# In the last stage of a one-core encoder step, the shift of every odd tile is added by GpSimd in place of VectorE

## The chip, the cores and the metric

The kernel runs on one core of one Trainium2 chip. The metric is the device time of one execution in microseconds (us); a measurement gives the median of several runs, and beside it one execution is recorded by the hardware profiler.

## What is computed

The reference is one inference step of a hybrid encoder layer for two request groups: a prompt of 2048 rows and a sample of 64 rows, each row 1024 float32 numbers wide. There is a modulated RMSNorm, one input projection to a state-space branch and a forgetting-attention branch, an output projection, a second modulated RMSNorm and a mixture of sixteen experts. After the layer comes a final modulated RMSNorm, and only that is touched here:

```
mod_p = (jax.nn.silu(c_prompt) @ w_ada_f + b_ada_f)[:, None, :]
sh_p, sc_p = jnp.split(mod_p, 2, axis=-1)
y_prompt = rmsnorm(yp, final_norm_w) * (1 + sc_p) + sh_p      # and the same for the sample group
```

So each row x of the layer's output becomes x * rs * scale + shift. Here rs is one over the root of the mean of the row's squares plus 1e-6, scale is final_norm_w * (1 + sc), and shift is sh. The scale and the shift are the same for all rows of one group.

## The kernel before

The kernel is a chain of stages (modulation, the state-space branch with the input projection, the forget sums, the projection to queries, keys and values, attention, output projection, routing, experts, `final`). Each stage is a block with one instruction stream per engine and semaphores between the streams. There is a barrier between stages, so `final` starts only when the experts have ended, and nothing follows it.

`final` works on 17 tiles of 128 rows (the last has 64), tile i = 0 to 16. SyncE's queue loads tile i into slot i % 8 of `x3` (L2437); from tile 8 on it first waits until the tile eight places earlier has been scaled. ScalarE squares the tile and sums the squares (`square`, L2449). VectorE makes the mean of one column (`mean`, L2477), ScalarE takes its root (L2454), and VectorE takes the reciprocal (L2482). VectorE then makes x * rs * scale into slot i % 4 of `out` (L2486, called the scaling here) and, after a wait on its own semaphore `scaled`, adds the shift in place (L2489, called the add). ScalarE's queue stores the slot to the result (`store`, L2459). The scaling of tile i waits until the store of tile i - 4 has landed, because it reuses its slot.

The scale rows and the shift rows lie in SBUF as `c.last_rows`. So the scaling has two whole tiles as inputs in SBUF (`x3` and the scale rows), and so has the add (`out` and the shift rows).

The order on each engine is written out by hand, and each engine works strictly in that order. The two loops that matter are:

```
# ScalarE
for i in range(NT):
    if i + 1 < NT:
        square(i + 1)
    take_root(i)
    if i >= 1:
        store(i - 1)
# VectorE
for i in range(NT):
    if i + 1 < NT:
        mean(i + 1)
    normalize(i)
```

A store waits on ScalarE for the add of its tile, so the square of the next tile but two stands behind that wait. GpSimd has no instruction in `final`.

Four other places of the kernel are spoken of because their rows show GpSimd and VectorE at work at once. In the state-space branch GpSimd makes `yskip` (L607) and `xw` (L611) and VectorE makes `xdt` (L683). In the forget sums GpSimd takes three of the differences `wb_lo` (L877) while VectorE runs sums along rows (L888 to L894). In attention GpSimd adds up `c_acc` (L1391), each time in place: accumulator plus a tile, all in SBUF and float32. In the experts GpSimd copies two numbers per row to `x_wg` (L2200).

Of the kernel before, what the change touches and what calls it, by code (L numbers as in the profile page):

```python
# [10 lines left out]
ALU = mybir.AluOpType  # L11
# [9 lines left out]
NT = NT_P + 1  # L21
# [31 lines left out]
def stage_semaphores(nc, ctx, prefix):  # L53

    handles = []

    def give_back():
        nc.clear_and_free_semaphores(handles)
        nc.all_engine_barrier()

    ctx.callback(give_back)

    def sem(name):
        handles.append(nc.alloc_semaphore(prefix + name))
        return handles[-1]

    return sem
# [7 lines left out]
def load_functions(nc, act, table):  # L75
    act.add_instruction(mybir.InstLoadActFuncSet(name=nc.get_next_instruction_name(), act_func_set_id=table, ins=[], outs=[]))
# [2340 lines left out]
def final(nc, c, a):  # L2417

    RING, RING_OUT = 8, 4
    with ExitStack() as ctx:  # L2420
        sb = lambda n, s, d=F32: ctx.enter_context(nc.sbuf_tensor("z_" + n, s, d))
        sem = stage_semaphores(nc, ctx, "z_")
        x3, out, junk = sb("x3", [P, RING, D]), sb("out", [P, RING_OUT, D]), sb("junk", [P, 2, D])
        st = sb("st", [P, NT, 4])
        ssq, ms, root, rs, scaled, out_ready = map(sem, ("ssq", "ms", "root", "rs", "scaled", "out_ready"))
        x_loaded, stored = [sem(f"x_loaded{s}") for s in range(RING)], [sem(f"stored{s}") for s in range(RING_OUT)]
        block = ctx.enter_context(nc.Block())
        rows_of = lambda i: P if i < NT_P else DEC
        group_of = lambda i: 0 if i < NT_P else 1

        @block.sync
        def _(sp):
            def load(i):
                n = rows_of(i)
                if i >= RING:
                    sp.wait_ge(scaled, i - RING + 1)
                sp.dma_start(x3[0:n, i % RING], c.x2[i * P:i * P + n, :]).then_inc(x_loaded[i % RING], 16)  # L2437

            for i in range(NT):
                load(i)  # L2440

        @block.scalar
        def _(act):
            load_functions(nc, act, SQRT)

            def square(i):
                n = rows_of(i)
                act.wait_ge(x_loaded[i % RING], 16 * (i // RING + 1))
                act.activation(junk[0:n, i % 2], x3[0:n, i % RING], ACT.Square, accum_out=st[0:n, i, 0:1]).then_inc(ssq, 1)  # L2449

            def take_root(i):
                n = rows_of(i)
                act.wait_ge(ms, i + 1)
                act.activation(st[0:n, i, 2:3], st[0:n, i, 1:2], ACT.Sqrt).then_inc(root, 1)  # L2454

            def store(i):
                act.wait_ge(out_ready, i + 1)
                dst = a["y_prompt"][0, i * P:(i + 1) * P, :] if i < NT_P else a["y_sample"][0]
                act.dma_start(dst, out[0:rows_of(i), i % RING_OUT]).then_inc(stored[i % RING_OUT], 16)  # L2459

            square(0)
# [6 lines that stand above are left out]
            store(NT - 1)  # L2468
            for s in range(RING_OUT):
                act.wait_ge(stored[s], 16 * len(range(s, NT, RING_OUT)))  # L2470

        @block.vector
        def _(dve):
            def mean(i):
                n = rows_of(i)
                dve.wait_ge(ssq, i + 1)
                dve.tensor_scalar(st[0:n, i, 1:2], st[0:n, i, 0:1], 1.0 / D, EPS, ALU.mult, ALU.add).then_inc(ms, 1)  # L2477

            def normalize(i):
                n, s, o, g = rows_of(i), i % RING, i % RING_OUT, group_of(i)  # L2480
                dve.wait_ge(root, i + 1)
                dve.reciprocal(st[0:n, i, 3:4], st[0:n, i, 2:3]).then_inc(rs, 1)  # L2482
                dve.wait_ge(rs, i + 1)
                if i >= RING_OUT:
                    dve.wait_ge(stored[o], 16 * (i // RING_OUT))
                dve.scalar_tensor_tensor(out=out[0:n, o], in0=x3[0:n, s], scalar=st[0:n, i, 3:4], in1=c.last_rows[0:n, g, 0, :],  # L2486
                                         op0=ALU.mult, op1=ALU.mult).then_inc(scaled, 1)
                dve.wait_ge(scaled, i + 1)
                dve.tensor_tensor(out[0:n, o], out[0:n, o], c.last_rows[0:n, g, 1, :], ALU.add).then_inc(out_ready, 1)  # L2489

            mean(0)
            for i in range(NT):
# [3 lines that stand above are left out]
# [6 lines left out]
def build(nc, a):  # L2502
    c = Shared()
    with ExitStack() as ctx:
# [45 lines left out]
        with ExitStack() as held:  # L2550
            weights = ExpertWeights(nc, held, a)
            routing(nc, c, a, weights)
            experts(nc, c, a, weights)
        final(nc, c, a)


# [28 lines left out]
```

## Time and profile before

| what | us |
|---|---|
| median of 3 runs | 2740.62 |
| lowest and highest of them | 2738.66, 2743.02 |
| the profiled execution, its own time | 2734.53 |
| its span from the first to the last instruction | 2732.8 |
| first load of `final` issued, by the span's clock | 2677.01 |
| last store of `final` issued | 2728.92 |

The profiled execution is a single one, and it was 6.09 us shorter than the median. The stage `final` takes the last 55.8 us of its span. Times inside the trace are given from the span's start; durations of one instruction are in us in an order of time and in ns where a view says mean or min/median/max. PE is TensorE, DVE is VectorE, ACT is ScalarE, POOL is GpSimd and SP is SyncE; a q behind a name is that engine's queue of issued transfers.

### The profile page before, as it was taken

The numbers are of one execution on the slowest core, as the hardware profiler recorded it, in microseconds if no ns is written. First come the engines' busy times: TensorE is split into PE (matmuls) and PEld (weight loads), VectorE is DVE, ScalarE is ACT, GpSimd is POOL, SyncE is SP. The second block draws the span as 40 slices with busy tenths as digits, with TensorE's granted clock in tenths as the row PEclk, the third lists the DMA queues.
The fourth block names the chain that finished last, engine by engine and source line by source line (L and its number), as shares of the span: only waits on it lengthen the run. The fifth ranks groups of instructions, "written<-read, shape, count | busy, mean of one in ns | idle before, by whom it ended". The sixth has DMA issues, their size and how long they took to land. (4 is left out here: it accounts for less than half of the span.)

```text
span 2732.8 us, 34773 instructions
## 1 busy us (share of the span) xinstructions
PE 2308.2 (84%) x11435; PEld 1788.9 (65%) x11436; DVE 1390.9 (51%) x2752; ACT 944.3 (35%) x1622; POOL 706.1 (26%) x753
## 2 busy tenths in 40 slices
PE   3799999739999979999995999708999999999870
PEld 1688888626778845556553888506888888888650
DVE  1488887761110056666663565531445662434556
ACT  1344444321111125555555343211223441223433
POOL 0010001020000057777774000051222222223220
PEclk8899999869999969999997999858999999999985
DMA  6421211146764294445522444315657776457656
GB/s 195 156 76 61 75 73 54 49 166 228 262 249 155 93 213 84 84 84 107 114 40 93 133 145 133 139 66 169 175 160 242 247 242 193 139 151 240 230 184 261
DMA packets 190201, 407.36 MB, mean 149 GB/s; under 512 B 65275, under 2 KB 72873, under 8 KB 186689
## 3 DMA queue, kind: packets, MB, share of 16 engines
q1 hardware_dynamic: 161152, 304.05, 34.6%
q0 software_dynamic: 26576, 93.53, 12.5%
q10 hardware_dynamic: 2384, 8.65, 0.8%
q8 instruction: 48, 0.79, 0.1%
q14 instruction: 41, 0.33, 0.0%
HBM read 296.12 MB, written 110.07 MB: 149 GB/s over the span
## 5 line engine op out<-in xcount | busy, mean ns | idle before, releaser
L1391 POOL TENSOR_TENSOR c_acc<-c_acc,c_pr 128x512 f32<-128x512 f32 (+3 forms) x320 | 340.4, 1064 | 73.4 <-ACT c_pr L1513 32.6
L1513 ACT ACTIVATE c_pr<-c_ps,neg_f 128x512 f32<-128x512 f32 (+2 forms) x360 | 207.8, 595 | 160.7 <-PE c_ps L1457 153.8
L1543 DVE TENSOR_REDUCE c_mx<-c_pm 128x1 f32<-128x512 f32 (+3 forms) x304 | 178.7, 613 | 57.4 <-PE c_pm L1413 39.4
L1413 PE MATMUL c_pm<-c_km,c_q 66*128 66x512 f32 (+1 forms) x336 | 143.8, 444 | 22.2 <-DMA c_km<-f_k 15.8
L258 PE MATMUL p_zx<-wa_hi,ah_hi 128*128 128x432 f32 x408 | 154.6, 379 | 3.6 <-DVE ah_lo L640 3.6
L258 PE MATMUL x_pg<-x_g_hi,x_x_hi 128*128 128x512 f32 x336 | 136.0, 405 | 23.9 <-DVE x_x_lo L2360 23.9
L1176 DVE SCALAR_TENSOR_TENSOR b_lo<-b_pu,b_hi 128x512 fp32r<-128x512 f32 (+1 forms) x40 | 24.5, 612 | 257.2 <-ACT b_hi L1145 257.2
L1466 PE MATMUL c_po<-c_pr,c_vv 128*64 128x512 f32 (+3 forms) x720 | 150.9, 521 | 0.0
L607 POOL TENSOR_TENSOR yskip<-xs,params 128x512 f32<-128x512 f32 x17 | 21.9, 1287 | 497.5 <-ACT xs L545 497.5
L259 PE MATMUL p_zx<-wa_lo,ah_hi 128*128 128x432 f32 x408 | 149.3, 366 | 0.0
L260 PE MATMUL p_zx<-wa_hi,ah_lo 128*128 128x432 f32 x408 | 148.6, 364 | 0.0
L258 PE MATMUL x_pd<-x_d_hi,x_m_hi 128*128 128x512 f32 x344 | 140.8, 409 | 6.8 <-DVE x_m_lo L2370 6.8
L2215 POOL DMA_INDIRECT x<-x_out,x_dst x43 | 75.5, 1755 | 268.1 <-DVE x_out L2378 262.3
L1451 PE MATMUL c_ps<-c_q,c_k 128*128 128x512 f32 (+2 forms) x360 | 135.9, 379 | 2.8 <-DMA c_vv<-in_cache_v_dram 2.8
L259 PE MATMUL x_pd<-x_d_lo,x_m_hi 128*128 128x512 f32 x344 | 137.3, 399 | 0.0
L260 PE MATMUL x_pd<-x_d_hi,x_m_lo 128*128 128x512 f32 x344 | 137.1, 399 | 0.0
L258 PE MATMUL x_pu<-x_u_hi,x_x_hi 128*128 128x512 f32 x336 | 136.5, 406 | 0.0
L1457 PE MATMUL c_ps<-c_q,c_k 97*128 97x512 f32 (+2 forms) x360 | 135.5, 378 | 0.5 <-DVE c_q L1569 0.5
L259 PE MATMUL x_pg<-x_g_lo,x_x_hi 128*128 128x512 f32 x336 | 135.2, 402 | 0.0
L260 PE MATMUL x_pg<-x_g_hi,x_x_lo 128*128 128x512 f32 x336 | 135.1, 402 | 0.0
L260 PE MATMUL x_pu<-x_u_hi,x_x_lo 128*128 128x512 f32 x336 | 133.3, 397 | 0.0
L259 PE MATMUL x_pu<-x_u_lo,x_x_hi 128*128 128x512 f32 x336 | 133.2, 396 | 0.0
(389 smaller groups left out, 5606.3 us busy)
## 6 DMA issues: line engine op xcount, KB each, us to landing
x_raw_g<-in_w_gate_dram SPq DMA_DIRECT2D x32, 1024.0 KB, 8.9
x_raw_u<-in_w_up_dram SPq DMA_DIRECT2D x32, 1024.0 KB, 7.3
x_raw_d<-in_w_down_dram SPq DMA_DIRECT2D x32, 1024.0 KB, 6.8
b_wa<-in_w_ada_dram POOLq DMA_DIRECT2D x16, 1024.0 KB, 7.6
c_k<-k_hi SPq DMA_DIRECT2D x14, 672.0 KB, 13.7
h_hi<-ah_hi SPq DMA_DIRECT2D x17, 512.0 KB, 2.6
h_lo<-ah_lo SPq DMA_DIRECT2D x17, 512.0 KB, 3.5
d_mix<-mix SPq DMA_DIRECT2D x17, 512.0 KB
```

Source lines behind the costliest of these rows:

```text
L258: pe.matmul(out, a_hi, b_hi, start=start, stop=False)
L259: pe.matmul(out, a_hi, b_lo, start=False, stop=False)
L260: return pe.matmul(out, a_lo, b_hi, start=False, stop=stop)
L1176: dve.scalar_tensor_tensor(out=lo[:, n % RING, 0:w], in0=bank_of(n)[:, 0:w], scalar=HD ** -0.5 if un["kind"] == "q" else 1.0, in1=hi[:, n ...
L1391: pool.tensor_tensor(acc[:, ci % 2, cols], acc[:, ci % 2, cols], pr[:, i % RING, cols], ALU.add).then_inc(acc_done, 1)
L1413: last = pe.matmul(p_m[x % 2][:, 0:w * P], q2[0:KR, s, u["tile"] * P:(u["tile"] + 1) * P], km[:, s, kc], start=True, stop=not masked)
L1451: pe.matmul(out[:, cols], k1[:, s, kc], q1[:, s, qc], start=True, stop=False)
L1457: pe.matmul(out[:, cols], k2[0:ROW + 1, s, kc], q2[0:ROW + 1, s, qc], start=False, stop=True).then_inc(s_done, 1)
L1466: pe.matmul(p_o[ci % 2][half * HD:(half + 1) * HD, cols], vv[:, it["h"] % 2, it["key"], :], pr[:, i % RING, cols], start=it["kb"] < 2, sto ...
L1513: act.activation(pr[:, n % RING, cols], p_s[n % NPS][:, cols], ACT.Exp, bias=c.neg_f[:, it["h"], it["key"]:it["key"] + 1]).then_inc(exp_do ...
L1543: dve.tensor_reduce(mx[:, u % 2, pc["slot"]:pc["slot"] + 1], src, AX.X, ALU.max).then_inc(mx_done, 1)
L2215: nc.gpsimd.indirect_dma_start(out=c.x2, out_offset=bass.IndirectOffsetOnAxis(ap=dst[:, 0:1], axis=0), in_=out[:], in_offset=None, compute ...
```

## The change

GpSimd gets a stream in `final`: for the odd tiles 1, 3, ..., 15 it waits until the tile is scaled and adds the shift in place, in the same slot of `out`. VectorE adds the shift for the nine even tiles alone. The one semaphore `out_ready` becomes two, one for each adder, and ScalarE's store waits for the one of its tile's parity. Loads, squares, roots, scalings, rings and the order on ScalarE stay as they were.

```
-        ssq, ms, root, rs, scaled, out_ready = map(sem, ("ssq", "ms", "root", "rs", "scaled", "out_ready"))
+        ssq, ms, root, rs, scaled = map(sem, ("ssq", "ms", "root", "rs", "scaled"))
+        shifted = [sem("shifted_dve"), sem("shifted_pool")]
...
             def store(i):
-                act.wait_ge(out_ready, i + 1)
+                act.wait_ge(shifted[i % 2], i // 2 + 1)
...
+        @block.gpsimd
+        def _(pool):
+
+            for i in range(1, NT, 2):
+                n, o, g = rows_of(i), i % RING_OUT, group_of(i)
+                pool.wait_ge(scaled, i + 1)
+                pool.tensor_tensor(out[0:n, o], out[0:n, o], c.last_rows[0:n, g, 1, :], ALU.add).then_inc(shifted[1], 1)
...
-                dve.wait_ge(scaled, i + 1)
-                dve.tensor_tensor(out[0:n, o], out[0:n, o], c.last_rows[0:n, g, 1, :], ALU.add).then_inc(out_ready, 1)
+                if i % 2 == 0:
+                    dve.wait_ge(scaled, i + 1)
+                    dve.tensor_tensor(out[0:n, o], out[0:n, o], c.last_rows[0:n, g, 1, :], ALU.add).then_inc(shifted[0], 1)
```

## Rows read from the trace of the kernel before

**Rows 1.** Windows of `final`: engines' busy us, granted clock, DMA share, GB/s.
```profile
2695.00:2700.00 5.00, 0.00 (x0) 0.00 (x0) 4.86 (x9) 2.05 (x7) 0.00 (x0) 0.50 1.03 422
...
2715.00:2720.00 5.00, 0.00 (x0) 0.00 (x0) 4.86 (x9) 2.48 (x6) 0.00 (x0) 0.50 0.47 192
```

**Rows 2.** Instructions of `final` by line and form: busy us, mean ns | idle before.
```profile
L2486 DVE SCALAR_TENSOR_TENSOR z_out<-z_x,z_st,last_rows 128x1024 f32<-128x1024 f32 x16 | 20.6, 1285 | 0.6
L2489 DVE TENSOR_TENSOR z_out<-z_out,last_rows 128x1024 f32<-128x1024 f32 x16 | 19.6, 1225 | 0.6
```

**Rows 3.** Timeline of one steady tile of `final`: start us, duration us.
```profile
2704.73 1.28 DVE L2486 SCALAR_TENSOR_TENSOR z_out<-z_x,z_st,last_rows 128x1024 f32<-128x1024 f32 x1
...
2706.05 1.22 DVE L2489 TENSOR_TENSOR z_out<-z_out,last_rows 128x1024 f32<-128x1024 f32 x1
2707.19 0.14 DVE L2477 TENSOR_SCALAR z_st<-z_st 128x1 f32<-128x1 f32 x1
2707.25 0.15 DVE L2482 RECIPROCAL z_st<-z_st 128x1 f32<-128x1 f32 x1
...
2707.44 1.28 DVE L2486 SCALAR_TENSOR_TENSOR z_out<-z_x,z_st,last_rows 128x1024 f32<-128x1024 f32 x1
2707.69 1.06 ACT L2449 ACTIVATE z_junk<-z_x 128x1024 f32<-128x1024 f32 x1 [1.47 <-DVE z_out L2489]
2708.65 0.19 ACT L2449 ACTIVATION_READ_ACCUMULATOR z_junk<-z_x 128x1 f32 x1
2708.74 0.19 ACT L2454 ACTIVATE z_st<-z_st 128x1 f32<-128x1 f32 x1
```

**Rows 4.** Waits within `final`: us in total, times, longest.
```profile
ACT z_junk L2449 <- DVE z_out L2489: 19.8, 14, 1.5
```

**Rows 5.** Attention, GpSimd's first adds, timeline.
```profile
974.95 1.00 POOL L1391 TENSOR_TENSOR c_acc<-c_acc,c_pr 128x384 f32<-128x384 f32 x1 [0.92 <-ACT c_pr L1513]
976.44 0.72 POOL L1391 TENSOR_TENSOR c_acc<-c_acc,c_pr 128x256 f32<-128x256 f32 x1 [0.49 <-ACT c_pr L1513]
980.38 0.45 POOL L1391 TENSOR_TENSOR c_acc<-c_acc,c_pr 128x128 f32<-128x128 f32 x1 [3.22 <-ACT c_pr L1513]
...
987.40 1.27 POOL L1391 TENSOR_TENSOR c_acc<-c_acc,c_pr 128x512 f32<-128x512 f32 x1 [1.11 <-ACT c_pr L1513]
```

**Rows 6.** State-space branch, GpSimd at two tiles, timeline.
```profile
147.50 1.21 POOL L607 TENSOR_TENSOR yskip<-xs,params 128x512 f32<-128x512 f32 x1 [23.69 <-ACT xs L545]
149.34 1.04 POOL L611 TENSOR_TENSOR xw<-xdt,e_out 128x512 f32<-128x512 f32 x1 [0.63 <-DVE xdt L683]
...
174.87 1.55 POOL L607 TENSOR_TENSOR yskip<-xs,params 128x512 f32<-128x512 f32 x1 [24.48 <-ACT xs L545]
```

**Rows 7.** The same two tiles, VectorE, timeline.
```profile
147.06 0.75 DVE L627 TENSOR_SCALAR xn<-x,st 128x1024 f32<-128x1024 f32 x1
147.73 1.53 DVE L683 TENSOR_TENSOR xdt<-xs,dt 128x512 f32<-128x512 f32 x1
...
174.82 0.69 DVE L683 TENSOR_TENSOR xdt<-xs,dt 128x512 f32<-128x512 f32 x1 [1.06 <-ACT xs L545]
```

**Rows 8.** All of L683: durations in ns, min/median/max.
```profile
L683 DVE TENSOR_TENSOR xdt<-xs,dt x17: 691/1532/1535, 121.2 to 549.8; 128x512 f32<-128x512 f32 x17
```

**Rows 9.** Forget sums: GpSimd's first difference, durations in ns.
```profile
L877 POOL TENSOR_TENSOR wb_lo_early<-wb_raw_early,wb_hi x1: 7646/7646/7646, 571.6 to 571.6; 128x1536 fp32r<-128x1536 f32 x1
```

**Rows 10.** Forget sums, VectorE in the same stretch, timeline.
```profile
571.58 4.41 DVE L888 TENSOR_TENSOR_SCAN f_sum<-f_ones,scratch 8x2048 f32<-8x2048 f32 x1
...
576.74 3.57 DVE L892 TENSOR_TENSOR_SCAN f_sum<-f_ones,f_clt 8x512 f32<-8x512 f32 x1
580.34 3.45 DVE L894 TENSOR_TENSOR_SCAN f_sum<-f_ones,f_sum,scratch 8x128 f32<-8x128 f32 x1
```

**Rows 11.** Attention, timeline: VectorE's product with one input outside SBUF, beside GpSimd.
```profile
1043.42 5.54 POOL L1391 TENSOR_TENSOR c_acc<-c_acc,c_pr 128x512 f32<-128x512 f32 x4 [1.19 <-ACT c_pr L1513]
...
1047.84 0.42 DVE L1588 TENSOR_TENSOR c_orow<-c_px,c_rinv 128x256 f32<-128x256 f32 x1
```

**Rows 12.** All of L1588: durations in ns, min/median/max.
```profile
L1588 DVE TENSOR_TENSOR c_orow<-c_px,c_rinv x38: 223/424/425, 1015.4 to 1454.2; 128x256 f32<-128x256 f32 x31, 128x64 f32<-128x64 f32 x7
```

**Rows 13.** Stores of `final`, from issue to landing.
```profile
DMA to landing us min/median/max: 2.6/4.5/7.7
```

## The prediction

> **What bounds the kernel now.** I read the windows of the last stage first. In its middle VectorE is busy 4.86 of every 5.00 us, ScalarE about 2.05 and GpSimd not at all. The transfers run at a DMA share of 1.03 and 422 GB/s there, but late in the stage they fall to 0.47 and 192 GB/s, and VectorE is as busy as before [rows 1]. The transfers are dense, then, but they don't set the pace. The list by line says what VectorE does: 16 whole-tile scalings at a mean of 1285 ns and as many adds at 1225 ns, with 0.6 us of idle time before each group [rows 2]. The timeline of one tile gives the beat. One scaling starts at 2704.73 and the next at 2707.44, so a tile takes 2.71 us, and VectorE's instructions fill it: scaling, add, a mean and a reciprocal of one column [rows 3]. A scaling ends at 2704.73 + 1.285 = 2706.015; from there to the start of the next are **1.425 us**, which hold the add. That is what the change takes away after each odd tile. The table of waits shows that ScalarE is not the bound: 14 of its squares wait for an add, 19.8 us in total [rows 4]. These waits exist because each store stands in ScalarE's order ahead of a square, and that will matter below.
>
> If the odd adds cost VectorE nothing, eight times about 1.26 us (1.425 less the 0.165 us from the end of the add at 2707.275 to the next scaling, which stay) would go, 10.1 us. The question is what a GpSimd add costs VectorE.
>
> **The change, part by part.**
>
> *GpSimd's add.* The stage has no GpSimd row, so its price comes from attention, where GpSimd adds float32 tiles in place in SBUF, as here. Standing alone, 128, 256, 384 and 512 columns take 0.45, 0.72, 1.00 and 1.27 us [rows 5]: a straight line, 0.273 us for each 128 columns. From 512 to 1024 columns that adds 4 x 0.273 = 1.09, so **2.36 us**. The low bound is twice the 1.04 us that a product of 512 columns with a repeated factor took [rows 6], 2.08 us; the high one is twice 1.27, 2.54 us. I take 2.36, since operation, types and placement agree. The Trainium skill's GPSIMD Engine Reference, section 3.1 on elementwise work, gives about 2.6 cycles an element for a two-input operation at 1.2 GHz; an estimate from it is 2.22 us, and by that the sum below would be 5.9 us in place of 7.0.
>
> *Can it run beside VectorE?* In the state-space branch GpSimd's L607 starts at 147.50 and ends at 148.71; VectorE's L683, which reads two SBUF tensors, starts at 147.73 and needs 1.53 us [rows 6, 7]. One tile later VectorE starts first, needs 0.69 us, and now GpSimd's instruction is the long one, 1.55 us [rows 6, 7]. The one that comes second is stretched to past the end of the first, and over all 17 tiles L683 lies between 691 and 1535 ns with the median at 1532 [rows 8]. In the forget sums GpSimd's first difference takes 7.646 us [rows 9] beside a VectorE sum that ends at 571.58 + 4.41 = 575.99; what is left after that end is 3.24 us. And there a VectorE sum of 128 columns takes 3.45 us, hardly less than one of 512 columns at 3.57 [rows 10]: both ended when GpSimd let go. By contrast L1588, which has one input outside SBUF, took 0.42 us in the middle of a run of GpSimd adds [rows 11], and never over 425 ns in 38 instances [rows 12]. So a GpSimd instruction on SBUF and a VectorE instruction with two SBUF inputs take turns. In this stage the scaling and the add of VectorE both have two SBUF inputs, and every GpSimd add reads two. I therefore expect no overlap with the large work: after the odd tile's scaling GpSimd adds, and the next scaling waits for it.
>
> *The sum for one pair of tiles.* GpSimd starts 0.08 us after VectorE's result (L683 ends at 149.26, L611 starts at 149.34) [rows 6, 7]. The add takes 2.36. A held instruction saves part of its start: L683 ended 0.55 us after GpSimd's end at 148.71, where alone it needs 0.69, so 0.14 is given back [rows 6 to 8]. Does GpSimd come first? The next scaling needs a mean and a reciprocal before it, at least 0.165 us, against 0.08, and if it did not, the add would be held instead, the sum of the turns being the same. So from one scaling's end to the next start, 0.08 + 2.36 - 0.14 = 2.30 us take the place of 1.425: **+0.875 us** a pair. The pairs are (1,2) to (15,16), eight, so **+7.0 us**. Bounds by the price of the add: 2.08 gives 8 x 0.595 = +4.8, 2.54 gives 8 x 1.055 = +8.4.
>
> *What else changes.* The odd store now waits 0.08 + 2.36 us after the scaling, and behind it on ScalarE stand a square and a root. In steady state VectorE still has 1.145 + 0.04 + 1.225 + 0.165 = 2.58 us to do after GpSimd's end, the held scaling and the even add, before it needs that square. ScalarE needs 1.66 us for it: from the end of an add at 2707.27 over store issue and square to the end of the root at 2708.93 [rows 3]. So VectorE's turn hides it with 0.7 us to spare, after allowing 0.2 for the reciprocal. The ring of four output slots: an odd store is issued when GpSimd ends, the scaling that reuses its slot comes two pairs of 6.30 later less 3.7, some 8.9 us, and the slowest store landed after 7.7 [rows 13]; hidden. Loads wait for scalings, which come later, so they only find emptier transfers. The second semaphore adds no wait on VectorE; it loses one on odd tiles. The last tile is even and VectorE adds it, so the tail after it stays.
>
> Against the profiled execution the sum is 2734.53 + 7.0 = 2741.5 (span 2739.8). The median of the runs lies 6.09 us above that execution; nothing in the change speaks to that gap, so I carry it: 2740.62 + 7.0 = **2747.6**.
>
> **The rivals.**
>
> *The two do overlap (not slower).* If whole tiles of 1024 columns were interleaved and not held, VectorE alone would be done early, but ScalarE's order then sets the beat: odd scaling 1.285, GpSimd 0.08 + 2.36, then store, square and root 1.66, reciprocal and start of the next scaling some 0.23 [rows 3, 5]: 5.615 us a pair against 5.42 now. That is 8 x 0.195 = +1.6, 2742.2: no change. Against it stand all the pairs of rows 6 to 10. It decides once the even scaling starts under 2.11 us (1.425 + 0.69, with 0.69 an eighth of 5.5) after the odd one's end, in place of 2.30. 0.12.
>
> *VectorE is relieved (faster).* For a gain over 0.2%, 0.69 a pair, that same ScalarE beat must come under 4.73, so the add under 4.73 - 3.255 = 1.48 us with no hold. At the limit it is 10.1 us, 2730.5. The line of rows 5 speaks against it: 0.03.
>
> *The small mean is held too (slower still).* The mean of one column has its input and output in SBUF; its square is done 1.57 us after the even add's end (2707.27 to 2708.84) [rows 3], and GpSimd starts after 0.165 + 1.285 + 0.08 = 1.53. If it has to wait for GpSimd, the scaling behind it is not ready to go: the 0.14 is lost and mean, reciprocal and start, 0.165, come after: 8 x 0.305 = +2.4 more, +9.4, 2750.0. No row shows a one-column VectorE instruction beside a GpSimd add. A one-input instruction with everything in SBUF was at work when the L607 of 1.21 us began [rows 6, 7], and that is no proof. 0.15. The Trainium skill's SBUF — State Buffer, section "Who interferes with whom", says that a tensor_scalar can run in a mode with both port pairs and then shuts GpSimd out or waits for it; by that rule this rival is the case, and the time would be 2750.0.
>
> **How the numbers follow.** The difference that a measurement can tell from none is about 0.2%, 5.5 us. My forecast, turns with the mean free, has 0.67; the other cases have 0.12, 0.03 and 0.15, and 0.03 is left for costs that no row shows, such as a first add that is slow behind the experts' indirect transfers. The forecast's bounds are 2745.4 and 2749.0, and the bar for slower lies inside them at 2746.1; with the runs' own spread of some 2 us I give 0.50 of its 0.67 to slower. With the mean's 0.15 and the 0.03 that is 0.68 slower. Same takes the other 0.17 and the 0.12, 0.29. Faster 0.03. The range has to hold the two larger cases and the add at its bounds: the highest is 8.4 + 2.4 = +10.8, 2751.4, widened by the spread to 2752; down to 2742 it reaches the overlapping case.
>
> **What would show it.** GpSimd's adds near 2.36 us, starting some 0.08 us after an odd scaling; the even scalings recorded much longer than 1285 ns, with the odd ones and the nine adds unchanged; pairs at 6.3 us. VectorE's idle time stays small, since held time counts as busy. If the mean is held, the long row is the mean and not the scaling. If the two overlap, even scalings stay at 1285 ns, VectorE idles, and its idle time ends with ScalarE's square or root. The prediction is wrong on its main step if even scalings are short, and wrong on its size alone if the add is far from 2.36 us.

## The result, and the profile after

The changed kernel took 2747.56 us in the median of 12 runs (2742.47 to 2750.99), the kernel before 2739.53 us (12 runs, 2738.19 to 2743.02): a ratio of 1.0027 with a 95% interval of 1.0018 to 1.0036, so it is slower, by 4.9 to 9.9 us.

The profiled execution of the changed kernel took 2745.86 us with a span of 2744.2, 11.4 more than the span before. Not all of that belongs to the change. The first load of the last stage was issued at 2681.82, against 2677.01 before, and nothing ahead of that point was changed; in the runs below it lies anywhere from 2677.19 to 2686.55. I therefore compare the **stage length**, from that issue to the end of the span: 2744.2 - 2681.82 = 62.4 us after, 55.8 before, **+6.6 us**.

By line and form, the last stage after (busy us, mean ns | idle before), to be read against [rows 2]:

```profile
L2495 DVE SCALAR_TENSOR_TENSOR z_out<-z_x,z_st,last_rows 128x1024 f32<-128x1024 f32 x16 | 32.9, 2059 | 0.6
L2479 POOL TENSOR_TENSOR z_out<-z_out,last_rows 128x1024 f32<-128x1024 f32 x8 | 18.7, 2340 | 46.1 <-DVE z_out L2495 46.1
...
L2499 DVE TENSOR_TENSOR z_out<-z_out,last_rows 128x1024 f32<-128x1024 f32 x8 | 9.8, 1226 | 0.3
```

VectorE lost eight whole-tile adds of 1.2 us, 9.8 us in all, and its 16 whole-tile scalings grew from 20.6 to 32.9 us, 12.3 us. A mean hides where: the timeline of one pair shows it (start us, duration us), to be read against [rows 3]:

```profile
2715.56 1.28 DVE L2495 SCALAR_TENSOR_TENSOR z_out<-z_x,z_st,last_rows 128x1024 f32<-128x1024 f32 x1
...
2716.92 2.34 POOL L2479 TENSOR_TENSOR z_out<-z_out,last_rows 128x1024 f32<-128x1024 f32 x1 [3.87 <-DVE z_out L2495]
2716.99 0.15 DVE L2486 TENSOR_SCALAR z_st<-z_st 128x1 f32<-128x1 f32 x1
2717.08 0.16 DVE L2491 RECIPROCAL z_st<-z_st 128x1 f32<-128x1 f32 x1
2717.28 3.06 DVE L2495 SCALAR_TENSOR_TENSOR z_out<-z_x,z_st,last_rows 128x1024 f32<-128x1024 f32 x1
2720.38 1.23 DVE L2499 TENSOR_TENSOR z_out<-z_out,last_rows 128x1024 f32<-128x1024 f32 x1
...
2721.77 1.28 DVE L2495 SCALAR_TENSOR_TENSOR z_out<-z_x,z_st,last_rows 128x1024 f32<-128x1024 f32 x1
```

The odd scaling takes its 1.28 us. GpSimd starts 0.08 us behind its end and adds until 2719.26. VectorE's mean and reciprocal of one column, next in its order, keep their 0.15 us. The even scaling starts at 2717.28 on paper but ends only at 2720.34, 1.08 us behind GpSimd. A pair takes 2721.77 - 2715.56 = 6.21 us, against 2 x 2.71 before. VectorE shows hardly any idle time; the time that it is held is booked as work of the held instruction. In the 5 us from 2715 (busy us of TensorE, its weight loads, VectorE, ScalarE and GpSimd, then granted clock, DMA share, GB/s) VectorE counts as busy for 4.78 of 5.00 us:

```profile
2715.00:2720.00 5.00, 0.00 (x0) 0.00 (x0) 4.78 (x7) 1.56 (x4) 2.34 (x1) 0.50 0.55 202
```

That is how such a loss looks in a profile: one instruction of a kind more than twice as long as its fellows (3.06 us against 1.28), and no idle time to show for it.

### The profile page after: what moved, and what is told of

Read it like the earlier page. It is cut to its first block and busy times, and to the rows that moved or that the text cites. A ratio compares the mean times of both kernels' runs of the same rounds, so it can differ in the third digit from the quotient of the medians.

```text
span 2744.2 us, 34773 instructions
## 1 busy us (share of the span) xinstructions
PE 2310.1 (84%) x11435; PEld 1789.9 (65%) x11436; DVE 1397.4 (51%) x2744; ACT 944.4 (34%) x1622; POOL 725.3 (26%) x761
```

## The experiments

The theory is that of the prediction: a GpSimd instruction that reads SBUF and a VectorE instruction with two SBUF inputs take turns (the turns theory). The rivals are that GpSimd's latency or ScalarE's order sets the beat, or that any GpSimd work holds VectorE. All stage lengths are counted in the same way, from profiled executions; the beat is that of one steady pair of tiles, from one odd scaling to the next. The kernels of e3, e4, e5 and e7 to e10 were executed once each, so their rows rest on one execution. Whole times of single executions are not compared: the issue of the stage's first load alone moves by 9.4 us among the runs. (The 2741.42 us of e4 are below every run of the changed kernel, but there the stage began at 2677.19 and was as long.)

| run | stage, us | pair, us | even scaling, us |
|---|---|---|---|
| before | 55.8 | 5.42 | 1.28 |
| after | 62.4 | 6.21 | 3.06 |
| e1_memset | 56.3 | 5.57 | 1.28 |
| e2_no_odd_add | 51.0 | 4.98 | 1.28 |
| e3_side_add | 70.5 | 7.26 | 3.12 |
| e4_order | 62.5 | 6.21 | 3.33 |
| e5_psum | 56.3 | 5.60 | 1.28 |
| e6_psum_order | 46.8 | 4.16 | 1.28 |
| e7_before_psum | 55.8 | 5.42 | 1.28 |
| e8_small_extra | 46.7 | 4.15 | 1.28 |
| e9_wide_extra | 57.9 | 5.55 | 1.28 |
| e10_before_order | 56.4 | 5.42 | 1.28 |

**e1_memset: GpSimd as busy, but only writing.**

```
-                pool.tensor_tensor(out[0:n, o], out[0:n, o], c.last_rows[0:n, g, 1, :], ALU.add).then_inc(shifted[1], 1)
+                pool.memset(spare[:], 0.0).then_inc(shifted[1], 1)      # spare: 2688 unused columns
```

> The add of the odd tiles is left out (their shift is missing); in its place GpSimd writes zeros into an unused tile of 2688 columns, which should take 2.3 us as the 64x2688 fills did, and the odd store waits for that. Stage length is counted from the issue of the first load of the last stage to the end of the span: 55.8 us before, 62.4 us after the change. Turns theory (GpSimd's reads of SBUF and VectorE's instructions with two SBUF inputs exclude each other): a fill reads nothing, so the even scalings stay at 1285 ns, ScalarE's order sets a beat of some 5.6 us a pair, stage 57 us. Rival (any GpSimd work of 2.3 us in this chain costs the same, by its delay or by holding VectorE): even scalings near 3.0 us or a beat of 6.2 us, stage 62 us.

The fill took 2.34 us, just as the add. Timeline of a pair:

```profile
2702.37 2.34 POOL L2480 MEMSET z_spare<- 128x2688 f32 x1 [3.23 <-DVE z_out L2496]
2703.14 1.28 DVE L2496 SCALAR_TENSOR_TENSOR z_out<-z_x,z_st,last_rows 128x1024 f32<-128x1024 f32 x1 [0.70 <-DMA out_y_prompt_dram<-z_out]
2704.46 1.22 DVE L2500 TENSOR_TENSOR z_out<-z_out,last_rows 128x1024 f32<-128x1024 f32 x1
```

The even scaling now runs wholly inside GpSimd's instruction and takes 1.28 us. The pair is 5.57 us, the stage 56.3, and the measured time is that of before (0.9997, interval 0.9987 to 1.0007). So GpSimd's presence and its latency in the chain of stores are not what costs; that it reads is what is left. With the hold gone ScalarE's order is the next bound, at the 5.6 us that the prediction had worked out for the overlapping case: from 2692 to 2735 VectorE's mean now waits for ScalarE's square nine times, where in the changed kernel it waited once (waits, us in total, times, longest; this run, then the changed kernel):

```profile
DVE z_st L2487 <- ACT z_junk L2451: 8.8, 9, 1.3
```

```profile
DVE z_st L2486 <- ACT z_junk L2450: 0.2, 1, 0.2
```

**e3_side_add: the reads alone, with nothing waiting for them.**

```
+        @block.gpsimd                                     # in the kernel before
+        def _(pool):
+            pool.memset(spare[:], 0.0).then_inc(spared, 1)
+            for i in range(1, NT, 2):
+                pool.wait_ge(spared, i // 2 + 1)
+                pool.wait_ge(scaled, i + 1)
+                pool.tensor_tensor(spare[:, 0], spare[:, 0], spare[:, 1], ALU.add).then_inc(spared, 1)
+            pool.wait_ge(spared, NT // 2 + 1)
```

> The kernel before, complete, and beside it GpSimd adds two unused tiles of 1024 columns once after each odd scaling; nothing waits for these adds inside the stage but its end. Turns theory: each add keeps VectorE's next two-input instruction waiting, 2.34 us less the 0.165 us of small instructions and about 0.2 us of saved start, so +2.0 us eight times, stage 71 to 72 us, and one scaling in two near 3.2 us. Rival (the change is slower because the odd store and ScalarE wait for GpSimd): nothing waits here, stage 55.8 us, scalings at 1285 ns.

```profile
2701.32 1.22 DVE L2500 TENSOR_TENSOR z_out<-z_out,last_rows 128x1024 f32<-128x1024 f32 x1
2701.43 3.32 POOL L2480 TENSOR_TENSOR z_spare<-z_spare 128x1024 f32<-128x1024 f32 x1 [3.94 <-DVE z_out L2497]
...
2702.71 3.12 DVE L2497 SCALAR_TENSOR_TENSOR z_out<-z_x,z_st,last_rows 128x1024 f32<-128x1024 f32 x1
```

Both sides are held in turn here. VectorE's add started 0.11 us ahead, so GpSimd's add waited for it and took 3.32 us instead of 2.34; then the scaling waited for GpSimd and took 3.12. The stage is 70.5 us, 14.7 more than before, 1.84 a pair; I had expected 71 to 72. Work on tiles that nobody needs costs VectorE what the change cost it, and more, since here no add was taken off it.

**e4_order: ScalarE's order.** In the changed kernel the store goes one tile later, with eight output slots:

```
-    RING, RING_OUT = 8, 4
+    RING, RING_OUT = 8, 8
-                if i >= 1:
-                    store(i - 1)
-            store(NT - 1)
+                if i >= 2:
+                    store(i - 2)
+            store(NT - 2)
+            store(NT - 1)
```

> The changed kernel, complete, with the stores one tile later in ScalarE's order and eight output slots in place of four, so that no square stands behind a wait for GpSimd. Turns theory: VectorE is still held for GpSimd's 2.34 us, stage 62 us, within 0.7, even scalings near 3.06 us. Rival (ScalarE's order behind the odd store sets the beat): stage at or under 56 us.

```profile
2700.03 2.34 POOL L2480 TENSOR_TENSOR z_out<-z_out,last_rows 128x1024 f32<-128x1024 f32 x1 [3.88 <-DVE z_out L2496]
...
2700.11 3.33 DVE L2496 SCALAR_TENSOR_TENSOR z_out<-z_x,z_st,last_rows 128x1024 f32<-128x1024 f32 x1
```

Stage 62.5, pair 6.21: unchanged. The even scaling starts earlier behind the odd one and is held for longer, to the same end (1.07 us behind GpSimd's). ScalarE's order is not the bound while VectorE is held.

**e2_no_odd_add: nothing on the odd tiles.**

```
-                pool.tensor_tensor(out[0:n, o], out[0:n, o], c.last_rows[0:n, g, 1, :], ALU.add).then_inc(shifted[1], 1)
+                pool.sem_inc(shifted[1], 1)
```

> The add of the odd tiles is left out altogether (their shift is missing); GpSimd only passes the signal on. Turns theory: nothing holds VectorE, the pair falls from 5.42 us by the 1.26 us of one add to 4.17 us, stage 55.8 - 10.1 = 46 us, all scalings 1285 ns; the transfers (17.33 MB at 420 GB/s, 41 us) should then be nearly the bound. Rival (the stage is bound elsewhere, by transfers or by ScalarE, so a relieved VectorE gains nothing): stage 54 to 56 us.

The stage is 51.0 us, between the two expectations and met by neither; the measured ratio is 0.9987 (0.9977 to 0.9996). The timeline names what took VectorE's place:

```profile
2702.97 1.28 DVE L2495 SCALAR_TENSOR_TENSOR z_out<-z_x,z_st,last_rows 128x1024 f32<-128x1024 f32 x1 [0.59 <-DMA out_y_prompt_dram<-z_out]
```

The scaling waits for the store that last used its slot. Four slots were enough at 5.42 us a pair; at 4.2 they are not.

**e5_psum and e6_psum_order: take VectorE's second input out of SBUF.** In the changed kernel the four rows of scale and shift are copied once into PSUM at the stage's start, two by VectorE and two by ScalarE, and VectorE reads them there. GpSimd's add is as in the change. The second run adds the edit of e4_order.

```
+        rows = ctx.enter_context(nc.psum_tensor("z_rows", [P, 2, 2, D], F32))
...
+            for r in range(2):
+                act.activation(rows[:, 1, r, :], c.last_rows[:, 1, r, :], ACT.Copy).then_inc(rows_in[1], 1)
...
+            for r in range(2):
+                dve.tensor_copy(rows[:, 0, r, :], c.last_rows[:, 0, r, :]).then_inc(rows_in[0], 1)
+            for q in range(2):
+                dve.wait_ge(rows_in[q], 2)
...
-                dve.scalar_tensor_tensor(out=out[0:n, o], in0=x3[0:n, s], scalar=st[0:n, i, 3:4], in1=c.last_rows[0:n, g, 0, :],
+                dve.scalar_tensor_tensor(out=out[0:n, o], in0=rows[0:n, g, 0, :], scalar=st[0:n, i, 3:4], in1=x3[0:n, s],
...
-                    dve.tensor_tensor(out[0:n, o], out[0:n, o], c.last_rows[0:n, g, 1, :], ALU.add).then_inc(shifted[0], 1)
+                    dve.tensor_tensor(out[0:n, o], out[0:n, o], rows[0:n, g, 1, :], ALU.add).then_inc(shifted[0], 1)
```

> The changed kernel, complete, with the scale and shift rows copied once into PSUM at the start of the stage, while the first loads are under way; VectorE's scalings and adds read them there and so have one SBUF input each, GpSimd's add is as in the change. Turns theory: GpSimd no longer holds VectorE, even scalings at 1285 to 1350 ns; then ScalarE's order behind the odd store sets the beat as with the fill, 5.6 us a pair, stage 56 to 57 us. Rival (GpSimd's reads of the output tile hold VectorE whatever VectorE's own inputs are): even scalings near 3.06 us, stage 62 us.

> The kernel of the run before with the stores one tile later in ScalarE's order and eight output slots in place of four, complete. Turns theory: with the hold gone and no square behind a wait for GpSimd, VectorE's own 4.2 us a pair or the transfers (17.33 MB at 420 GB/s, 41 us) set the pace, stage 46 to 50 us, 6 to 10 us faster than the kernel before, 0.997. Rival (the slots or GpSimd's 2.34 us in the chain keep it): stage 54 us or more, no change.

Timeline of a pair in e6_psum_order:

```profile
2700.36 1.28 DVE L2500 SCALAR_TENSOR_TENSOR z_out<-z_rows,z_st,z_x 128x1024 f32<-128x1024 f32 x1
...
2701.73 2.35 POOL L2484 TENSOR_TENSOR z_out<-z_out,last_rows 128x1024 f32<-128x1024 f32 x1 [1.81 <-DVE z_out L2500]
2701.81 1.28 DVE L2500 SCALAR_TENSOR_TENSOR z_out<-z_rows,z_st,z_x 128x1024 f32<-128x1024 f32 x1
...
2703.13 1.22 DVE L2504 TENSOR_TENSOR z_out<-z_out,z_rows 128x1024 f32<-128x1024 f32 x1
...
2704.52 1.28 DVE L2500 SCALAR_TENSOR_TENSOR z_out<-z_rows,z_st,z_x 128x1024 f32<-128x1024 f32 x1
```

The even scaling and most of the even add lie inside GpSimd's add, and each takes the time that it takes alone. With the PSUM rows alone the pair is 5.60 us and the stage 56.3, as with the fill, and VectorE's mean again waits for ScalarE's square (8 times, 8.1 us in total from 2692 to 2735): ScalarE's order. With order and slots changed too the pair falls to 4.16 us and the stage to 46.8. Measured, e6_psum_order takes 2730.92 us against 2740.82, a ratio of 0.9964 (0.9950 to 0.9977): it beats the kernel before, and its slowest run, 2735.22, lies under the changed kernel's fastest, 2742.47. Its windows (columns as above) show the next bound:

```profile
2700.00:2705.00 5.00, 0.00 (x0) 0.00 (x0) 4.86 (x11) 2.88 (x7) 2.35 (x1) 0.50 1.03 420
...
2720.00:2725.00 5.00, 0.00 (x0) 0.00 (x0) 4.86 (x8) 0.20 (x1) 2.84 (x2) 0.50 1.02 419
```

VectorE is still full, and now the transfers stay dense until 5 us before the end of the span, where before they had fallen off [rows 1].

**e7_before_psum and e10_before_order: the parts without GpSimd.** The first is the kernel before with the PSUM rows, the second the kernel before with the order and the eight slots.

> A control: the kernel before, complete, with the scale and shift rows in PSUM and nothing else changed, so no GpSimd. Turns theory: PSUM rows do nothing by themselves without GpSimd beside them, stage 55.8 us, within 0.7, scalings at 1285 to 1350 ns and adds at 1225 to 1300. Rival (an input in PSUM is itself faster and would explain a gain of the two runs before it): scalings clearly under 1285 ns and a stage under 55 us.

> A control: the kernel before, complete, with the later stores and eight output slots alone; no GpSimd, rows in SBUF. Turns theory: VectorE's 2.71 us a tile stay the pace, stage 55.8 us, within 0.7. Rival (the gain of the combined run came from order and slots): stage under 52 us.

The stages are 55.8 and 56.4 us, with the pair at 5.42 in both. Neither part gains anything by itself. In the first, scalings have a mean of 1285 ns and adds of 1221: an input in PSUM leaves the scaling as it was and the add 4 ns shorter.

```profile
L2490 DVE SCALAR_TENSOR_TENSOR z_out<-z_rows,z_st,z_x 128x1024 f32<-128x1024 f32 x16 | 20.6, 1285 | 0.6
L2493 DVE TENSOR_TENSOR z_out<-z_out,z_rows 128x1024 f32<-128x1024 f32 x16 | 19.5, 1221 | 0.6
```

**e8_small_extra and e9_wide_extra: does a one-input instruction wait too?** In e6_psum_order one more instruction follows each even scaling, in the middle of GpSimd's add:

```
+                    dve.tensor_scalar(spare[:, i // 2, 0:1], c.last_rows[:, 0, 0, 0:1], 0.5, 1.0, ALU.mult, ALU.add)   # e8; 0:D in e9
```

> The run with PSUM rows, the later stores and eight slots, complete, with one more VectorE instruction behind each even scaling: a tensor_scalar of one column from SBUF to an unused SBUF tile. There GpSimd's add has run for some 1.4 of its 2.35 us. If a one-input instruction of one column goes by freely: 0.15 us as the means, pair 4.3 us, stage 47 to 48 us. Rival (such an instruction, with all in SBUF, waits for GpSimd too): it ends with GpSimd's add, about 1.1 us long, pair 5.2 us, stage 52 to 55 us.

> The same with the extra tensor_scalar on 1024 columns, which alone took 0.75 us in the state-space branch. By the Trainium skill's page SBUF - State Buffer, section Who interferes with whom, a tensor_scalar in SBUF can use both port pairs and then waits for GpSimd: by that rule it would take about 1.6 us, from 1.4 us into the add to some 0.6 us behind its end. Turns theory in its narrow form (two SBUF inputs are needed): 0.75 us, pair 4.9 us, stage 51 to 53 us. Rival (every wide SBUF instruction is held): 1.6 us, pair 5.8 us, stage 57 to 60 us.

The small one (durations in ns, min/median/max, then its place in the timeline), and the wide one in the same way:

```profile
L2504 DVE TENSOR_SCALAR z_spare<-last_rows x9: 134/143/145, 2688.9 to 2722.3; 128x1 f32<-128x1 f32 x9
```

```profile
2700.11 2.35 POOL L2485 TENSOR_TENSOR z_out<-z_out,last_rows 128x1024 f32<-128x1024 f32 x1 [1.81 <-DVE z_out L2501]
...
2701.40 0.14 DVE L2504 TENSOR_SCALAR z_spare<-last_rows 128x1 f32<-128x1 f32 x1
```

```profile
L2504 DVE TENSOR_SCALAR z_spare<-last_rows x9: 684/1605/1669, 2689.2 to 2732.6; 128x1024 f32<-128x1024 f32 x9
```

```profile
2703.64 2.34 POOL L2485 TENSOR_TENSOR z_out<-z_out,last_rows 128x1024 f32<-128x1024 f32 x1 [3.21 <-DVE z_out L2501]
...
2704.93 1.60 DVE L2504 TENSOR_SCALAR z_spare<-last_rows 128x1024 f32<-128x1024 f32 x1
```

One column passes freely, 1.3 us into GpSimd's add, at 143 ns. The wide one ends at 2706.53, 0.55 us behind GpSimd's end at 2705.98, and takes 1.60 us where the first of the nine, with no GpSimd beside it, took 0.684. The narrow form of my theory (two SBUF inputs are needed) is wrong for it.

The trace of the kernel before already held a sign of this, which the prediction did not use. In the forget sums a one-input tensor_scalar of 2688 columns stands beside GpSimd's third difference:

```profile
583.49 3.53 POOL L877 TENSOR_TENSOR wb_lo_early<-wb_raw_early,wb_hi 128x1536 fp32r<-128x1536 f32 x1
```

```profile
583.83 4.59 DVE L896 TENSOR_SCALAR f_sum<-f_sum 8x2688 f32<-8x2688 f32 x1
```

It takes 4.59 us and ends 1.40 us behind GpSimd. Scaled up from the 0.684 us of 1024 columns it would take some 1.8 us alone, an estimate.

## Why the prediction was right

*Turns.* It is the main step, and it holds. The even scaling is held with GpSimd reading (after, e3) and free with GpSimd only writing (e1) or with VectorE's second input in PSUM (e5, e6). For the scaling and the add both ingredients are needed, and each alone is harmless. The rule is too narrow, though: a wide instruction with one input is held as well (e9). And only GpSimd adds with two SBUF inputs were tried, so what one with a single input does is open. In the forget sums the two short VectorE sums did not both end when GpSimd let go, as the prediction reads them: the first ended 1.08 us behind the end of GpSimd's first difference, the second 0.27 us behind the end of the second (579.19 + 4.33 = 583.52). That leaves them a case of turns, only less neatly.

*The price of GpSimd's add.* 2.36 us was drawn out along the line of [rows 5]; the eight took 2340 ns on average. Twice the product with a repeated factor, 2.08, was short. The Trainium skill's GPSIMD Engine Reference, section 3.1 on elementwise work, gives about 2.6 cycles an element for a two-input operation at 1.2 GHz; the estimate of 2.22 us from it was short as well.

*The start and the part given back.* GpSimd's start came 0.08 us behind the scaling's end, as priced. A held scaling gives back more than the 0.14 taken from L683: it ends 1.08 us behind GpSimd where alone it needs 1.285, so 0.20. From the odd scaling's end to the even one's start in effect are then 0.08 + 2.34 - 0.20 = 2.22 us, not 2.30, and the pair costs 6.21 - 5.42 = 0.79 us more, not 0.875. Eight pairs make +6.3 where the sum said +7.0; with 0.3 us from the stage's ends (0.16 of it ahead of the first scaling) it is the +6.6 of the stage. That lies inside the measured 4.9 to 9.9; the medians differ by 8.0, and no run shows a cause for the other 1.4 us. That the forecast of 2747.6 met the median of 2747.56 to the tenth is chance: it started from 2740.62, 1.1 above the 2739.53 of all 12 runs, and added 7.0, 1.0 less than the medians differ by, and the two misses cancel.

*What was called hidden.* ScalarE's square and root behind the odd store: hidden, as e4 shows, which changed nothing. The ring of four slots: hidden at this beat, but not at 4.98 us a pair (e2).

*The rivals.* The overlapping case did not occur, but its price was good: 5.615 us a pair, and 5.57 and 5.60 where the hold was taken away (e1, e5). VectorE relieved, 10.1 us, is near what e6 got (1.26 us a pair, 9.0 us in the stage, 9.9 in the median), with three edits beside the change: an input out of SBUF, another order on ScalarE, more slots. The order and the slots were only tried together, so the share of each is not shown. The small mean held: it was not held in the change, where it started 0.07 us behind GpSimd, and e8 shows it free in the middle of an add. The Trainium skill's SBUF — State Buffer, section "Who interferes with whom", which the prediction named beside that rival, says that a tensor_scalar can contend with GpSimd. The wide tensor_scalar agrees with it (1.60 us against 0.684); the one of a single column did not wait.

## What to carry to other kernels

Before work is moved from VectorE to GpSimd, ask what each reads: if VectorE's neighbouring instructions have two whole tiles in SBUF as inputs (or are a wide tensor_scalar with one) and GpSimd adds tiles in SBUF, the two run in turns, and the slower engine's time (2.34 us for an add that VectorE does in 1.23) is paid almost in full, 2.22 us here. Look in the trace for places where both already work at once; a duration with a median at twice its minimum, as in [rows 8], is a sign. Moving VectorE's constant operand to PSUM made the same move pay, once the order on ScalarE and the number of output slots were changed too.

## What the runs showed of the hardware

A one-input tensor_scalar of 1024 columns with all in SBUF is held by a GpSimd add, to 0.55 us behind its end, while one of a single column is not (143 ns); what lies between was not tried. The hold goes both ways: in e3 GpSimd's add was held as well, for 3.32 us in place of 2.34, behind a VectorE add that had started 0.11 us ahead. A GpSimd fill of 2.34 us did not disturb VectorE's scaling at all (1276 to 1286 ns over all 17). And an operand in PSUM cost VectorE nothing at 1024 float32 columns: 1285 ns for a scaling and 1221 for an add, against 1285 and 1225.
